# Mixer of a hybrid encoder block: a new order of work on every engine, from the first normalization to the router

## The reference, cut to what matters

```python
h = rmsnorm(x) * norm_mix
proj = h @ w_in                      # 1024 x 8224: q, k, v, gate of 8 heads; low-rank gates; branch gates
# heads 0..3 (retention): q, k rotated by position (rope); chunks of 128 rows
scores = (q @ k.T) * decay_mask      # in each chunk, both directions
out = scores @ v + (q * decay) @ state        # state: running sum of k.T @ v over the chunks
# heads 4..7 (gated linear attention): the same with data-dependent decays
#   la = log_sigmoid(low_rank @ gate_w + gate_b) / 16, cumulated in the chunk, then exp
out = normalize(out) * norm * silu(gate)      # per head
merged = sigmoid(g0) * (ret @ w_branch_ret) + sigmoid(g1) * (gla @ w_branch_gla)
x = x + merged @ w_out
h = rmsnorm(x) * norm_ffn
affinity = softmax(h @ w_router)     # 16 experts
gate, idx = top_k(affinity.T, 128)   # each expert takes 128 rows
x = x + scatter(experts(h[idx]) * gate)       # 16 experts: 1024 -> 2816 -> 1024, silu gated
return rmsnorm(x) * norm_final
```

## Time and profile before

| | us |
|---|---|
| time, median of 3 runs (3050.96 to 3053.57) | 3053.51 |
| the profiled execution's own time | 3055.88 |
| its span, first to last instruction | 3054.0 |
| PE busy (share of the span) | 2763.2 (90%) |
| DVE busy | 1938.5 (63%) |
| ACT busy | 1635.8 (54%) |
| POOL busy | 214.9 (7%) |

### The profile page before, as it was taken

One profiled execution on the slowest core, in us unless ns is written; L12 is line 12 of the kernel. 1 busy time (PEld: TensorE's weight loads), 2 busy tenths in 40 slices (PEclk: granted clock), 3 DMA queues, 4 the chain that ended last, 5 costly groups with the idle time before them and its releaser, 6 DMA issues. The chain is left out here.

```text
span 3054.0 us, 36906 instructions
## 1 busy us (share of the span) xinstructions
PE 2763.2 (90%) x13530; PEld 2357.4 (77%) x13530; DVE 1938.5 (63%) x1974; ACT 1635.8 (54%) x1542; POOL 214.9 (7%) x232
## 2 busy tenths in 40 slices
PE   3898899988989899995199999999999999999994
PEld 2787787777777787774188888888888888888884
DVE  6334242534435232423888988888888989888885
ACT  5232322533334222222177777787877777777874
POOL 0000100101010101100000000000000000000000
PEclk8899999989999999996599999999999999999997
DMA  3121533412052434424299999999999999999995
GB/s 104 31 75 53 93 63 62 69 44 90 28 90 56 117 68 108 137 94 178 97 353 381 382 384 375 385 375 384 390 375 383 378 384 385 378 375 385 378 376 191
DMA packets 254613, 691.41 MB, mean 226 GB/s; under 512 B 18465, under 2 KB 75809, under 8 KB 254529
## 3 DMA queue, kind: packets, MB, share of 16 engines
q1 hardware_dynamic: 229680, 626.73, 55.1%
q0 software_dynamic: 24848, 63.52, 9.9%
HBM read 635.66 MB, written 54.53 MB: 226 GB/s over the span
## 5 line engine op out<-in xcount | busy, mean ns | idle before, releaser
L1643 DVE TENSOR_TENSOR e_part<-e_raw,e_part 128x2048 fp32r<-128x2048 f32 (+2 forms) x576 | 1197.1, 2111 | 193.2 <-ACT e_part L1593 192.0
L1593 ACT ACTIVATE e_part<-e_raw 128x2048 fp32r<-128x2048 f32 (+2 forms) x576 | 1009.1, 1773 | 319.1 <-PE e_y_ps L1765 171.2
L105 PE MATMUL m_proj<-m_hT,m_w_part 128*128 128x512 f32 (+1 forms) x2352 | 567.8, 400 | 33.4 <-DVE m_qd L783 23.6
L105 PEld LDWEIGHTS m_proj<-m_hT,m_w_part 128*128 128x128 f32 (+1 forms) x2352 | 445.4, 190 | 137.0 <-issue 35.3
L1785 PE MATMUL e_gate_ps<-e_part,e_xgT 128*128 128x512 f32 (+1 forms) x2304 | 496.8, 373 | 1.5 <-DVE e_xgT L1648 1.5
L1765 PE MATMUL e_y_ps<-e_part,e_actT 128*128 128x512 f32 x2112 | 497.6, 392 | 0.0
L1785 PE MATMUL e_up_ps<-e_part,e_xgT 128*128 128x512 f32 (+1 forms) x2304 | 489.0, 371 | 0.0
L1785 PEld LDWEIGHTS e_gate_ps<-e_part,e_xgT 128*128 128x128 f32 x2304 | 423.0, 189 | 62.8 <-issue 1.9
L1785 PEld LDWEIGHTS e_up_ps<-e_part,e_xgT 128*128 128x128 f32 x2304 | 421.7, 188 | 59.8
L1765 PEld LDWEIGHTS e_y_ps<-e_part,e_actT 128*128 128x128 f32 x2112 | 392.8, 188 | 79.2
L752 DVE TENSOR_TENSOR m_w_part<-m_w_raw,m_w_part 128x1024 fp32r<-128x1024 f32 (+1 forms) x97 | 116.9, 1214 | 343.6 <-ACT m_w_part L474 343.6
(11 more groups left out here) (225 smaller groups left out, 1876.0 us busy)
## 6 DMA issues: line engine op xcount, KB each, us to landing
e_raw<-in_w_down_dram SPq DMA_DIRECT2D x160, 1024.0 KB, 8.0
e_raw<-in_w_gate_dram SPq DMA_DIRECT2D x128, 1024.0 KB, 7.5
e_raw<-in_w_up_dram SPq DMA_DIRECT2D x128, 1024.0 KB, 8.6
e_raw<-in_w_gate_dram SPq DMA_DIRECT2D x64, 768.0 KB, 8.8
e_raw<-in_w_up_dram SPq DMA_DIRECT2D x64, 768.0 KB, 5.9
m_w_raw<-in_w_in_dram SPq DMA_DIRECT2D x64, 512.0 KB, 4.3
ret_sum<-m_stage POOLq DMA_DIRECT2D x64, 256.0 KB, 4.7
gla_sum<-m_stage POOLq DMA_DIRECT2D x64, 256.0 KB, 4.1
```

Source lines behind the costliest of these rows:

```text
L105: last = nc.tensor.matmul(out, x_at(x[xi], kc), w_at(w[wi], kc), start=start and kc == 0 and (xi, wi) == (0, 0), stop=stop and kc == chunk ...
L1593: nc.scalar.activation(part[k % PARTS][0][:, 0:size(k)], raw[k % RAW][:, 0:size(k)], ACT.Copy).then_inc(w_high, 1)
L1643: nc.vector.tensor_tensor(part[k % PARTS][1][:, 0:size(k)], raw[k % RAW][:, 0:size(k)], part[k % PARTS][0][:, 0:size(k)], ALU.subtract).th ...
```

## The change

- **Start.** The first DMA brings only the identity and the gain. The gain is made a row with two matmuls (`spread_gain`, unit M) so that `norm_x` applies it, and each half tile of `hT` is written by one instruction per engine instead of four. Roots are taken in groups of 1, 1, 2 and 4 tiles. The A units are interleaved with turning tiles 4 to 7, and `take_first_qk` copies their banks to SBUF at once; rope is applied later by `rope_first`. The tables are built between.
- **Heads.** v tiles follow the branch units from E3 on. In a retention head K, v 6, v 7 and Q come before E12 to E15; in a gated head Q is two pairs with E12 and E13 between them. VectorE reads the scores before the splits of the next blocks. Scores go to other places in SBUF (`probs_ret`, `probs_gla`). The last high part of a head (`high_of_flip(hd, 3)`) comes after the first `take_sum` of the next.
- **Gates.** The four Z products stand among the A units of the next head (`middle_of`). ScalarE reads Abs directly from PSUM, VectorE folds each bank, and Exp and Ln come before the root of the head.
- **Merge.** The tail interleaves four E units, then R and pairs of E.
- **Output.** 12 blocks O instead of 16: left half of tiles 0 to 3, then of 4 to 7, then the right half of all tiles with its four blocks resident (a fourth slot lies in `stage`), tile by tile, each tile's root, normalization and router product following it. Only `norm_mid(7)` stays behind the softmax.
- **Hand-over.** The wait for the stores moves from the end of `mixer` to the SP and POOL queues of `experts`.

The core of the diff:

```diff
     HD, SLOTS, RAW = 2 * HEADS, 3, 2
+    GROUPS = ((0, 1), (1, 2), (2, 4), (4, NT))
+    MID_GROUPS = ((0, 2), (2, 4), (4, 6), (6, 7), (7, 8))
...
+    def middle_of(hd):
+
+        if hd + 1 < HD:
+            fill = [("A", hd + 1, i) for i in range(4)]
+        else:
+            fill = [("R", 0, i) for i in range(4)]
+        s = [("S", hd, i) for i in range(NT - 1)]
+        z = [("Z", hd + 1, i) for i in range(4)]
+        if hd == 0:
+            return [fill[0], *s[0:2], fill[1], *s[2:4], fill[2], *s[4:7], fill[3]]
...
+        if HEADS <= hd + 1 < HD:
+            return [*s[0:2], fill[0], *s[2:4], fill[1], *s[4:6], z[0], fill[2], s[6], z[1], fill[3], *z[2:4]]
+        return [*s[0:2], fill[0], *s[2:4], fill[1], *s[4:6], fill[2], s[6], fill[3]]
...
+    slot_of = [n % SLOTS for n in range(len(blocks) - 4)]
+    slot_of += [SLOTS] + slot_of[-3:]
...
-            sp.dma_start(x_sb[:, 0, :], x[0, 0:P, :]).then_inc(x_in[0], 16)
-            sp.dma_start(cst[:], consts).then_inc(const_in, 16)
-            sp.dma_start(mix_gain[:], norm_mix).then_inc(const_in, 16)
-            for t in range(1, NT):
+            sp.dma_start(cst[:, 0:P], consts[:, 0:P]).then_inc(gain_in, 16)
+            with nc.allow_non_contiguous_dma(reason="a column of gains"):
+                sp.dma_start(mix_gain[:], norm_mix).then_inc(gain_in, 16)
+            for t in range(NT):
                 sp.dma_start(x_sb[:, t, :], x[0, t * P:(t + 1) * P, :]).then_inc(x_in[t], 16)
...
+            def take_first_qk(i):
+
+                u = ("A", 0, i)
+                w, half = qk_order(0)[i]
+                at = slice(half * HALF, half * HALF + HALF)
+                scale, h0 = 1.0 if w else QK_SCALE, DK // 2
+                wait_proj(act, u)
+                nc.scalar.activation(swapped_sb[0:h0, 2 * w + half, :], proj_bank(u)[h0:DK, :], ACT.Copy, scale=scale)
+                nc.scalar.activation(swapped_sb[h0:DK, 2 * w + half, :], proj_bank(u)[0:h0, :], ACT.Copy, scale=scale
+                                     ).then_inc(swapped, 1)
+                proj_took(nc.scalar.activation((qd, kd)[w][:, 0, at], proj_bank(u)[:], ACT.Copy, scale=scale), u)
...
                 if hd:
-                    for u in range(16):
+                    for u in range(12):
                         take_sum(hd - 1, u)
-                        if gla and u in (1, 3, 5, 7):
-                            decay_exps(hd, u // 2)
+                        if u == 0:
+                            high_of_flip(hd - 1, 3)
                         if u == 7:
                             split_high()
...
+                if hd:
+                    split_low()
                 if is_ret(hd):
                     weigh_rows(hd)
                 else:
                     for k in range(2):
                         weigh_near(hd, k)
+                split_low()
...
+                take_scores(hd, 0)
                 split_low()
+                take_scores(hd, 1)
                 split_low()
                 if hd:
                     split_low()
...
+                    for t in range(6):
+                        branch(hd - 1, 2 * t)
+                        branch(hd - 1, 2 * t + 1)
+                        if t:
+                            project_v(hd, t - 1)
+                    project_v(hd, 5)
+                    if is_ret(hd):
+                        turn_keys(hd, 0)
+                        turn_keys(hd, 1)
+                        project_v(hd, 6)
+                        project_v(hd, 7)
+                        score(hd, 0)
+                        score(hd, 1)
+                        for i in range(12, 16):
+                            branch(hd - 1, i)
...
+            for t in range(NT):
+                for kb in range(4):
+                    multiply(2, kb, t)
+                    if t and kb == 2:
+                        turn_mid(t - 1, 1)
+                        if t + 1 < NT:
+                            turn_mid(t + 1, 0)
+                if t:
+                    for c in range(2):
+                        route(t - 1, c)
+            route(NT - 1, 0)
+            turn_mid(NT - 1, 1)
+            route(NT - 1, 1)
...
+            for s, n in mid_stored:
+                sp.wait_ge(s, n)
             for k in range(RAW):
                 load(0, k)
```

More of the change, by code:

```diff
@@ L343, in rope_count, with probs_of, turned @@
         def rope_count(hd, w, half):
[L344 removed]
+            return 4 * hd + (2 * w + 2 if hd == 0 else 2 * w + half + 1)
+        def probs_of(hd):
+            return probs_ret if hd < HEADS - 1 else probs_gla
+        def turned(hd):
+            return range(2 if is_ret(hd) else 4)
         block = ctx.enter_context(nc.Block())
@@ L628, in _ @@
+                    if not gla:
+                        take_keys(hd)
+                    take_v(hd, 3)
+                    split_high()
+                    split_high()
+                    for u in range(12, 16):
+                        take_sum(hd - 1, u)
+                    split_high()
+                else:
+                    for m in range(2):
+                        take_v(hd, m)
                     split_high()
-                    for m in range(3):
+                    for m in range(2, 4):
@@ new lines, in _ @@
+                for u in middle_of(hd):
+                    if u[0] == "A":
+                        take_qk(nxt, u[2])
+                    elif u[0] == "R":
+                        light(u)
+                    elif u[0] == "L":
+                        at = slice(u[2] * HALF, (u[2] + 1) * HALF)
+                        wait_proj(act, u)
+                        proj_took(nc.scalar.activation(low_rank[0:2 * RANK, at], proj_bank(u)[0:2 * RANK, :], ACT.Copy), u)
+                    elif u[0] == "Z":
+                        read_gate(nxt, u[2])
+                    if u[0] in "AR" and u[2] % 2 or u == ("L", 0, 1):
+                        split_high()
@@ L988, in _ @@
             third = 2 * np.pi - first - second
-            for piece in (first, second, third):
-                chain.link(nc.vector.scalar_tensor_tensor(out=ang, in0=turns, scalar=-piece, in1=ang,
-                                                          op0=ALU.mult, op1=ALU.add))
-            cosine, over = curve[:, 0, :], tmp[:, 1, :]
-            chain.link(nc.vector.tensor_scalar(cosine, ang, np.pi / 2, None, ALU.add))
-            chain.link(nc.vector.tensor_scalar(over, cosine, np.pi, -2 * np.pi, ALU.is_gt, ALU.mult))
@@ new lines, in take_turns, with bound_angles @@
+            def take_turns(*pieces):
+                for piece in pieces:
+                    chain.link(nc.vector.scalar_tensor_tensor(out=ang, in0=turns, scalar=-piece, in1=ang,
+                                                              op0=ALU.mult, op1=ALU.add))
+            def bound_angles():
+                chain.link(nc.vector.tensor_scalar(cosine, ang, np.pi / 2, None, ALU.add))
+                chain.link(nc.vector.tensor_scalar(over, cosine, np.pi, -2 * np.pi, ALU.is_gt, ALU.mult))
+                chain.link(nc.vector.tensor_tensor(cosine, cosine, over, ALU.add))
+                bound = float(np.nextafter(np.float32(np.pi), np.float32(0)))
+                nc.vector.tensor_scalar(curve[:], curve[:], bound, -bound, ALU.min, ALU.max).then_inc(angles_done, 1)
@@ new lines, in _ @@
+            nc.vector.memset(ones[:], 1.0).then_inc(ones_ready, 1)
+            dve.wait_ge(gain_in, 32)
+            for kc in range(KC):
+                ins = nc.vector.tensor_scalar(diag[:, kc, :], ident, mix_gain[:, kc:kc + 1], None, ALU.mult)
+            ins.then_inc(diag_done, 1)
+            root_of_x(0)
+            root_of_x(1)
+            for u in (("M", 0, 0), ("M", 0, 1)):
+                wait_proj_taken(dve, u)
+            norm_x(0)
+            norm_x(1)
+            root_of_x(2)
@@ new lines, in _ @@
+            h_low_of(0)
+            norm_x(2)
+            h_low_of(1)
+            norm_x(3)
+            split_low()
+            h_low_of(2)
+            h_low_of(3)
+            split_low()
+            root_of_x(3)
+            norm_x(4)
+            norm_x(5)
+            h_low_of(4)
+            norm_x(6)
+            h_low_of(5)
+            norm_x(7)
+            h_low_of(6)
+            h_low_of(7)
+            whole_turns()
+            split_low()
+            take_turns(first, second)
@@ L998, in _ @@
+            split_low()
+            decay_rates()
+            take_turns(third)
+            bound_angles()
             dve.wait_ge(act_tables, 3)
+            for w in range(2):
+                rope_first(w)
             nc.vector.memset(low_rank[2 * RANK:2 * RANK + 1, :], 1.0)
@@ L1122, in _ @@
             nc.vector.tensor_tensor(logit[:], logit[:], wide(peak[:, 2, :]), ALU.mult).then_inc(softmaxed, 1)
-            for t in range(4, NT):
-                norm_mid(t)
+            norm_mid(NT - 1)
         @block.tensor
@@ L1386, in route @@
```

(5 more changed lines are left out.)

749 lines of the change are left out of this document (395 added, 354 removed).

## The result

The changed kernel takes 2869.04 us (median of 4 runs, 2868.20 to 2870.29) against 3052.85 for the kernel before (4 runs, 3050.96 to 3053.57): a ratio of 0.9399, 95% interval 0.9383 to 0.9415, faster. The forecast was 2875.0, range 2858 to 2915. The profiled execution took 2869.58, its span is 2867.6; I compare spans, 3054.0 with 2867.6, a difference of 186.4 (by medians 183.8).

What follows compares the result with a forecast made beforehand. PE was taken to bound the mixer, its waits costing run time; DMA and PE fill the unchanged experts stage. Terms -39.7, -108.3, -26.9 and -3.6 sum to -178.5, giving a median of 2875.0 us, range 2858 to 2915.

Steps and rivals of the forecast that it cites:

- Start: Up to the first v tile: from 99.11 to 59.4 us, -39.7, nearly all gained behind the opening; bounds -25 and -46.
- gains land near 5.4: In the opening: the gain arrives near 5.4 us, so the first tile is normalized at about 12.3 instead of 9.6.
- Heads and merge: From first v tile to output projection: 89.3 us idle and 27 of slow clock go, 8 of new waits come; -108.3.
- I take 8 for all: In the heads: all new waits of PE together cost 8 us, with 1 us at head 0.
- Scores are read before the splits and E12 to E15 cover: In the heads: early reads, and PE's branch units E12 to E15 (4 x 1.4 us) cover reads of 1.28 or 1.84.
- Output projection: From 142.4 to 115.5 us, -26.9: 107.8 to the last product, then a tail of about 7.7.
- Hand-over: One `norm_mid` of 1.22 us instead of four (4.86) ahead of the last store: -3.6; moving the wait: 0 or -1.
- Rival 1: In the heads: splits replace scores as the wait, two waits of 3 us a head over 7 heads; 2933; chance 0.14.
- Rival 2: In the start: gain row, roots and longer normalizations queue on DVE, so it gives only -25; 2890; chance 0.11.
- Rival 3: More gain than forecast: no new wait and the opening at its lower bound; 2861; chance 0.10.
- Rival 4: Slower than before: `stage` copies wait for sums in DRAM; needs 25.5 us a head; chance 0.02.
- The table load: Between `stage` copies in gated heads: 1.28 us; with a 1.38 drain E3 would wait 1.4 in four heads, 5.5 more.

Runs made afterwards that it cites:

- banks_held: Changed kernel, but ScalarE copies the four first q and k banks, with the splits that hang on them, only after the tables; 2895.59 us, ratio 0.9489.
- whole_constants: Changed kernel, but the first transfer brings all 452 KB of constants instead of the 64 KB of the identity; 2870.34 us, ratio 0.9407.
- output_phase: Kernel before with only the new output phase and hand-over; start, heads, gates and merge as they were; 3017.73 us, ratio 0.9889.
- norms_behind: Changed kernel with `norm_mid` of tiles 4 to 7 behind the softmax and x_mid stores ahead of h_mid stores; 2873.72 us, ratio 0.9418.
- wait_back: Changed kernel with the waits for the stores back at the end of SyncE's mixer queue; 2870.27 us, ratio 0.9406.
- exps_ahead: Changed kernel, but in gated heads ScalarE does the far exponentials of direction 1 before the split that E8 needs; 2880.83 us, ratio 0.9441.
- scores_first: Kernel before with one change: VectorE reads a head's scores ahead of the three splits; 2991.51 us, ratio 0.9805.

## Why the prediction was right

The forecast erred by 6.0 us of 184 by medians, and by 7.9 (178.5 for 186.4) by the spans that its terms are made of. Every term had the right sign, and no rival came in. Point by point:

- **Start, -39.7 forecast, -42.3 measured.** The mechanism was right: the A banks are free at once and the tables lie under the v tiles (banks_held: the first v tile 24.7 later without it). Mis-sized was "gains land near 5.4": they are there by 2.98. I had put the new small transfers behind the 4.63 us of an x tile instead of ahead of it. The first normalization starts those 2.4 us earlier than forecast, and so do the first A unit (2.4) and the first v tile (2.5). That the gain is the cause is read from the chain of the forecast against the trace; whole_constants doesn't isolate it, since it holds back x too. (The forecast's own sum is loose by 0.1 or 0.2: its terms give 59.2, it says 59.3 and goes on with 59.4.) The matmul of 512 columns at 1.9 was right (3.78 for both halves), as was the forecast that the opening itself gains little (3.9 us to the first A unit, 29.71 to 25.81) and the rest comes from behind it.
- **Heads and merge, -108.3 forecast, -112.3 measured.** Idle time 89.3 to 3.3, slow clock 26.3 for my 27. The step that was mis-sized is "I take 8 for all" the new waits: 3.3 in all, of which 1.0 is in head 0 and 1.78 in the merge tail, where I had looked for none. The seven E8 places cost what I had as their lower end, 0.2 each, and mostly not as listed idle time. Much of the 4.0 by which the stage beat the forecast may lie in the trace of before: in output_phase, whose heads and merge are those of before less the 2.9, the stage takes 1175.34 us (98.72 to 1274.06), 3.4 less than 1181.60 less 2.9.
- **What the sum did not tell.** "Scores are read before the splits and E12 to E15 cover" named two measures for one loss. The sum counted the loss once, so it came out right, but it gave no share to either. The four kernels do: without both, +78.9; without the cover, +13.3; without the early read, +0.6 in the span and +2.4 in the stage. I had expected +6 to +10 for the last, because I looked at where the read ends and not at when TensorE next needs the bank.
- **Output projection, -26.9 forecast, -27.4 measured,** and the tail 7.15 for my 7.7. Alone on the kernel before it gives 27.0.
- **Hand-over, -3.6 forecast, -4.0 measured,** shown by norms_behind; the moved wait is worth nothing, as forecast (wait_back).
- **Rival 1** is a real mechanism at 3.2 us a gated head (exps_ahead, 12.7 in the stage for four): 2.0 of wait and 1.2 of slower matmuls. I had priced a wait at 3 and the slow clock at 2.3 for two of them, so about 4.2 a wait, which is too much. What I argued against it, that the split is ahead of the exponentials in ScalarE's order, is what decides. **Rival 2** did not come: the opening queues on VectorE as followed, only earlier. **Rival 3**, 2861, wanted no new wait and a start of 53 us; the waits went most of the way to it and the start two fifths of it. **Rival 4** did not come: the only wait for a `stage` copy, 1.78, is due to a split in ScalarE's queue, and no instruction is listed as waiting for a sum.
- **The table load.** The Trainium skill, "ScalarE: Activation LUTs", section "What ACT_TABLE_LOAD costs", adds a drain of 1.38 us to a switch of tables. In the trace of the changed kernel the load takes 1.28 us and its exponential starts at once (726.97), with no drain between, so the trace disagrees and the measurement decides. The place that I had named was wrong: not E3 but E4 comes behind that load. With 0.6 to 0.7 us to spare, the drain would have made E4 wait by about 0.7 us in four heads (an estimate from that figure and the trace), 3 in the sum and not 5.5.

What stays open: what a later gain costs alone, and where the 3.4 us went that the heads of before took longer in the profiled execution than in that of output_phase.

## What to carry to other kernels

When the trace shows an engine waiting for a late read, look at both ends of the wait: what stands ahead of the read in the reader's queue, and what the waiting engine could run meanwhile. Either cure may be enough; cure one, measure, and take the second only for its own remainder. Price an idle tensor engine with the slow clock behind it: here each wait of 7 to 12 us cost 2.0 us more. In a strict queue, put the instruction that may have to wait for another engine (a split that needs a slot) behind those whose result that engine needs next.

## What the runs showed of the hardware that I had not expected

- The first small transfers land early: identity (64 KB) and gain (4 KB), issued ahead of the x tiles, are there by 2.98 us; behind 452 KB of constants the instruction that waits for the gain starts only 1.27 us later (4.25), and the first x tile is the more delayed of the two (its square 1.77 later).
- The windows' clock column gives 1.00 in the opening of the changed kernel, but at 25.81 twelve matmuls of 512 columns take 5.11 us, and from 45.85 forty-eight take 11.16 (2.8 for twelve). In the opening the durations tell the speed and the column does not.
- A wait of 1.6 us slows the states behind it hardly (2.10 and 2.11 for eight, 1.89 in the earlier trace rows); waits of 5.18 (scores_first, head 7) and of 8.35 double them (3.78 and 3.75).
